# Down-projection: two of four weight block sums by adding transfers, two alternating block pairs, products in another order, and one more turn by products

## The reference, cut to what matters

```python
D_MODEL, SEQ, D_FF = 2048, 256, 5632
u_gate, u_val = u[..., :D_FF], u[..., D_FF:]
x = x + jnp.einsum('bsf,fd->bsd', jax.nn.silu(u_gate) * u_val, w_down[l])
```

## Time and profile before

| What | Value |
|---|---|
| Device time, median of 3 | 2073.01 us (2072.57 to 2073.12) |
| The profiled execution | 2072.76 us, its span 2070.8 us |
| TensorE matmul busy | 2065.6 us of 2070.8 |
| VectorE busy | 1639.7 us (79%) |
| ScalarE busy | 1162.5 us (56%) |
| GpSimd busy | 50.2 us (2%) |
| DMA queue of SP | 394.66 MB, 55.9% of 16 engines' span |
| DMA queue of GpSimd | 18.88 MB, 5.3% |
| Granted TensorE clock | 1.000 |

### The profile page before, as it was taken

How to read it: one execution, slowest core, us unless ns; L and a number is a source line. 1 busy time by engine, 2 the same in 40 slices (tenths; PEclk the granted TensorE clock), 3 DMA queues, 4 the chain that set the end, 5 groups by cost and what they waited for, 6 DMA issues and landing times.

```text
span 2070.8 us, 25481 instructions
## 1 busy us (share of the span) xinstructions
PE 2065.6 (100%) x9908; PEld 1734.6 (84%) x9908; DVE 1639.7 (79%) x1846; ACT 1162.5 (56%) x1387; POOL 50.2 (2%) x53
## 2 busy tenths in 40 slices
PE   9999999999999999999999999999999999999999
PEld 8888888888888887888888888888888888888887
DVE  7988888887888876886788668867777777789986
ACT  6766555555556555665555455555555555555553
POOL 0000000000000000110000000000000000000000
PEclk9999999999999999999999999999999999999999
DMA  9667777787774766655465556455555555556663
GB/s 344 210 200 220 226 232 225 211 245 220 247 262 151 224 207 215 204 157 189 140 231 180 201 184 221 156 185 182 191 186 192 192 193 184 193 182 235 223 206 130
DMA packets 117719, 423.28 MB, mean 204 GB/s; under 512 B 13152, under 2 KB 13920, under 8 KB 117344
## 3 DMA queue, kind: packets, MB, share of 16 engines
q1 hardware_dynamic: 109440, 394.66, 55.9%
q0 software_dynamic: 5184, 18.88, 5.3%
q10 hardware_dynamic: 2976, 8.14, 1.1%
HBM read 419.52 MB, written 2.10 MB: 204 GB/s over the span
## 4 chain that ended last, share of the span: by engine, by line
PE 99%; DMA 0%; ACT 0%; DVE 0%; ACTq 0%; issue 0%; DVEq 0%
PE g L905 52%; PE xs L951 9%; PE xs L772 8%; PE g L772 8%; PE g L955 7%; PE g L743 4%; PE xs L778 4%; PE g L778 4%; PE xs L821 1%; PE xs L992 1%; PE xs L1125 0%; PE g L930 0%; PE xs L1122 0%; DMA par<-in_params 0%; PE xs L1139 0%; PE xs L1069 0%
## 5 line engine op out<-in xcount | busy, mean ns | idle before, releaser
L1809 DVE TENSOR_TENSOR w_lo<-raw,w_hi 128x1024 fp32r<-128x1024 f32 x631 | 765.3, 1222 | 307.0 <-ACT w_hi L1322 299.6
L1322 ACT ACTIVATE w_hi<-raw 128x1024 fp32r<-128x1024 f32 x631 | 661.7, 1057 | 530.7 <-PE g L905 232.5
L905 PE MATMUL g<-w_hi,in_both 128*128 128x512 f32 x1104 | 350.6, 390 | 0.0
L905 PE MATMUL g<-w_hi,mid_both 128*128 128x512 f32 x992 | 320.3, 393 | 0.0
L905 PEld LDWEIGHTS g<-w_hi,in_both 128*128 128x128 f32 x1104 | 207.3, 188 | 42.9
L905 PEld LDWEIGHTS g<-w_hi,mid_both 128*128 128x128 f32 x992 | 186.3, 188 | 38.5
L905 PE MATMUL g<-w_lo,in_both 128*128 128x512 f32 x552 | 214.8, 389 | 0.0
L905 PE MATMUL g<-w_lo,mid_both 128*128 128x512 f32 x496 | 193.1, 389 | 0.0
L772 PE MATMUL g<-mlp_both,w_hi 128*128 128x512 f32 x704 | 167.0, 391 | 0.0
L772 PE MATMUL xs<-mlp_both,w_hi 128*128 128x512 f32 x704 | 165.6, 390 | 0.0
L772 PEld LDWEIGHTS xs<-mlp_both,w_hi 128*128 128x128 f32 x704 | 130.7, 188 | 26.2
(11 more groups left out here) (507 smaller groups left out, 3347.0 us busy)
## 6 DMA issues: line engine op xcount, KB each, us to landing
raw<-in_stream SPq DMA_DIRECT2D x631, 512.0 KB, 4.2
d_block<-in_stream SPq DMA_DIRECT2D x28, 512.0 KB, 4.3
o_block<-in_stream SPq DMA_DIRECT2D x24, 512.0 KB, 4.9
v_block<-in_stream SPq DMA_DIRECT2D x20, 512.0 KB, 4.4
ge_block<-in_stream POOLq DMA_DIRECT2D x15, 512.0 KB, 5.4
gm_block<-in_stream SPq DMA_DIRECT2D x12, 512.0 KB, 6.1
ge_block<-in_stream SPq DMA_DIRECT2D x10, 512.0 KB, 4.5
gl_block<-in_stream POOLq DMA_DIRECT2D x6, 512.0 KB, 5.4
```

The costliest lines, as they stand in the source:

```text
L905: ins = mm(GG[:, bank, :], a[:, kt, t * P:(t + 1) * P], w[:, slot, half_chunk(j)], start=n == 0 and opens(item, bank), stop=ended and n == ...
L1322: activation(w_hi[:, n % RING, :], of[:], ACT.Copy).then_inc(hi_ready, 1)
L1809: v.tensor_tensor(w_lo[:, n % RING, :], of, w_hi[:, n % RING, :].bitcast(F32), ALU.subtract).then_inc(lo_ready, 1)
```

## The change

It changes the stage `down` alone. (1) `down` joins `SPREAD`: VectorE makes two of a quad's sums (B11 + B12, and at product 2 B11 + B21 with B21 from the ring); the two with B22 are made by adding transfers that GpSimd issues. Products 3 and 2 take their blocks from the ring. (2) The four `d_block` buffers become two pairs (B11, B12) that alternate between quads; block loads are issued two quads ahead, with semaphores of their own for the second pair. (3) The order of a mixed turn becomes `MIXED_SPREAD`. (4) In group 1 turn 10 goes by products too, interleaved with the chunks of turn 8; turn 7's chunks are interleaved with the products of turn 6. Its activation sums are made at item 76, those of turn 6 still at item 64. The stage has 112 items where it had 109.

```diff
-             ((3, 0), (7, None), (4, 1), (5, 2), (8, 6), (9, None), (10, None))),
+             ((3, 0), (4, 1), (5, 2), (7, 6), (8, 10), (9, None))),
...
-SUM_TURNS = {"v": (3, 2), "out1": (4, 5), "vv": (0,), "down": (0, 1, 2, 6), "gm0": (3, 2), "out2": (1,)}
+SUM_TURNS = {"v": (3, 2), "out1": (4, 5), "vv": (0,), "down": (0, 1, 2, 6, 10), "gm0": (3, 2), "out2": (1,)}
...
-SUMS_AT = {"v": (4, 8), "out1": (2, 6), "vv": (-7,), "down": (3, 7, 11, 64), "gm0": (-8, -5), "out2": (-7,)}
+SUMS_AT = {"v": (4, 8), "out1": (2, 6), "vv": (-7,), "down": (3, 7, 11, 64, 76), "gm0": (-8, -5), "out2": (-7,)}
...
-SPREAD = ("ug", "vv", "side")
+SPREAD = ("ug", "vv", "side", "down")
+TWO_SUMS = ("vv", "side", "down")
...
 MIXED = (1, "C0", 5, 7, "C1", 6, 3, "C2", 4, 2, "C3")
...
+MIXED_SPREAD = (1, "C0", 5, "C1", 7, "C2", 6, 3, 2, "C3", 4)
...
-             FIRST_ITEM["down"] + 13: ("down", B22), FIRST_ITEM["down"] + 14: ("down", B21),
+             FIRST_ITEM["down"] + 13: ("down", B11, 1), FIRST_ITEM["down"] + 14: ("down", B12, 1),
...
+def second_pair(q):
+
+    return QUADS[q][0] == "down" and (q - quads_ahead("down")) % 2 == 1
...
 def buffer_of(q, b):
 
+    if QUADS[q][0] == "down":
+        return b + 2 * second_pair(q)
...
             for n, item in enumerate(ITEMS):
-                if next_in_place(item) is not None and quad_of(item) + 1 < len(QUADS):
-                    q = quad_of(item)
-                    if QUADS[q + 1][0] == item.phase:
+                after = 2 if item.phase == "down" else 1
+                if next_in_place(item) is not None and quad_of(item) + after < len(QUADS):
+                    q = quad_of(item) + after
+                    if QUADS[q][0] == item.phase:
                         sp.wait_ge(lo_ready, n + 1)
-                        load_block(q + 1, next_in_place(item))
+                        load_block(q, next_in_place(item))
...
-                    if item.phase in MID_ORDER and item.product == 2:
+                    if item.phase in TWO_SUMS and item.product == 2:
 
                         sp.wait_ge(sem["block_sums"], sums_made(quad_of(item), 4))
...
-                elif item.phase in MID_ORDER and item.product == 2:
+                elif item.phase in TWO_SUMS and item.product == 2:
                     dve.wait_ge(lo_ready, n + 1)
-                    to = wide(item.phase, item.group).blocks[B11]
+                    to = wide(item.phase, item.group).blocks[buffer_of(quad_of(item), B11)]
                     v.tensor_tensor(to[:], to[:], raw[:, CHUNK_COUNT[n] % RING, :], ALU.add).then_inc(sem["block_sums"], 1)
...
-                p.dma_start(wide(item.phase, item.group).blocks[to][:], stream[block_row(q, b)], accum_op=ALU.add).then_inc(
+                p.dma_start(wide(item.phase, item.group).blocks[buffer_of(q, to)][:], stream[block_row(q, b)], accum_op=ALU.add).then_inc(
```

More of the change, by code:

```diff
@@ L174 @@
         for _turn, _by_products in _steps:
-            for _what in (PLAIN if _by_products is None else MIXED_LATE if _name in ("gm1", "out2") else MIXED):
+            _mixed = MIXED_LATE if _name in ("gm1", "out2") else MIXED_SPREAD if _name in SPREAD else MIXED
+            for _what in PLAIN if _by_products is None else _mixed:
                 if _what in PLAIN:
@@ L277, in loads_of_block @@
 def loads_of_block(q, b):
-    return sum(phase not in SPREAD or b in (B11, B12) for phase, _, _ in QUADS[:q + 1])
+    return sum(not second_pair(k) and (QUADS[k][0] not in SPREAD or b in (B11, B12)) for k in range(q + 1))
+def second_pair(q):
+    return QUADS[q][0] == "down" and (q - quads_ahead("down")) % 2 == 1
 def spread_quads(q):
@@ L305, in sums_made @@
 def sums_made(q, p):
-    ahead = sum(1 if phase == "ug" else 2 if phase in MID_ORDER else 4 for phase, _, _ in QUADS[:q])
-    return ahead + ({5: 1, 4: 2} if QUADS[q][0] in MID_ORDER else {5: 1, 7: 2, 6: 3, 4: 4})[p]
+    ahead = sum(1 if phase == "ug" else 2 if phase in TWO_SUMS else 4 for phase, _, _ in QUADS[:q])
+    return ahead + ({5: 1, 4: 2} if QUADS[q][0] in TWO_SUMS else {5: 1, 7: 2, 6: 3, 4: 4})[p]
 def buffer_of(q, b):
+    if QUADS[q][0] == "down":
+        return b + 2 * second_pair(q)
     return b if b == B21 or QUADS[q][0] in SPREAD else (b + q - quads_ahead(QUADS[q][0])) % 3
@@ L569, in build @@
     down_wide = Wide(sb, "d", [("mix", 0), ("mix", 4 * kib), ("y", 88 * kib), ("y", 92 * kib)],
-                     [("h", 0), ("h", 4 * kib), ("h", 8 * kib), ("y", 12 * kib)],
-                     [("h", 12 * kib), ("h", 16 * kib), ("h", 20 * kib), ("y", 56 * kib)], ("h", 24 * kib), ("h", 28 * kib),
+                     [("h", 0), ("h", 4 * kib), ("h", 8 * kib), ("y", 12 * kib), ("y", 16 * kib)],
+                     [("h", 12 * kib), ("h", 16 * kib), ("h", 20 * kib), ("y", 56 * kib), ("y", 60 * kib)], ("h", 24 * kib), ("h", 28 * kib),
                      ("h", 24 * kib))
@@ L633, in build, with block_in @@
     block_full = [sem[f"block_full{b}"] for b in range(4)]
+    second_full = [sem[f"second_full{b}"] for b in (B11, B12)]
+    def block_in(q, b):
+        if second_pair(q):
+            return second_full[b], 16 * ((q - quads_ahead("down")) // 2 + 1)
+        return block_full[b], 16 * loads_of_block(q, b)
     hi_ready, lo_ready, mm_done = sem["hi_ready"], sem["lo_ready"], sem["mm_done"]
@@ L668, in load_block @@
                 phase, g, _ = QUADS[q]
-                sp.dma_start(wide(phase, g).blocks[buffer_of(q, b)][:], stream[block_row(q, b)]).then_inc(block_full[b], 16)
+                sp.dma_start(wide(phase, g).blocks[buffer_of(q, b)][:], stream[block_row(q, b)]).then_inc(block_in(q, b)[0], 16)
             for n, item in enumerate(ITEMS):
-                if next_in_place(item) is not None and quad_of(item) + 1 < len(QUADS):
-                    q = quad_of(item)
-                    if QUADS[q + 1][0] == item.phase:
+                after = 2 if item.phase == "down" else 1
+                if next_in_place(item) is not None and quad_of(item) + after < len(QUADS):
+                    q = quad_of(item) + after
+                    if QUADS[q][0] == item.phase:
                         sp.wait_ge(lo_ready, n + 1)
-                        load_block(q + 1, next_in_place(item))
+                        load_block(q, next_in_place(item))
                 if in_ring(item) and CHUNK_COUNT[n] + RING < len(CHUNK_ITEMS):
@@ L711, in _ @@
                         sp.wait_ge(sem["y_ready"], GROUPS)
-                    load_block(QUADS.index((phase, of[0], MID_TURN)) if of else quads_ahead(phase), b)
+                    if of and phase == "down":
+                        load_block(quads_ahead(phase) + of[0], b)
+                    else:
+                        load_block(QUADS.index((phase, of[0], MID_TURN)) if of else quads_ahead(phase), b)
                 if n in GAIN_AT:
@@ L1309, in high_of_chunk @@
                     if item.product in (1, 3, 2):
-                        act.wait_ge(block_full[b], 16 * loads_of_block(q, b))
-                    elif item.phase in SPREAD and item.product != 5 and not (item.phase in MID_ORDER and item.product == 4):
+                        act.wait_ge(*block_in(q, b))
+                    elif item.phase in SPREAD and item.product != 5 and not (item.phase in TWO_SUMS and item.product == 4):
                         act.wait_ge(sem[f"block_added{item.product}"], 16 * spread_quads(q))
@@ L1422, in first_product @@
                             act.wait_ge(sem["own_read"], own_ahead(phase, g))
-                            act.wait_ge(sem["sums_lo_ready"], sums_ahead(phase) + 4)
+                            act.wait_ge(sem["sums_lo_ready"], sums_ahead(phase) + 5)
                         own = own_banks(phase, g)
@@ L1820, in block_sums @@
                     q = quad_of(item)
-                    dve.wait_ge(block_full[B11], 16 * loads_of_block(q, B11))
-                    dve.wait_ge(block_full[B12], 16 * loads_of_block(q, B12))
+                    dve.wait_ge(*block_in(q, B11))
+                    dve.wait_ge(*block_in(q, B12))
                     dve.wait_ge(lo_ready, n + 1)
                     block_sum(item, B11, B12, B11)
-                elif item.phase in MID_ORDER and item.product == 2:
+                elif item.phase in TWO_SUMS and item.product == 2:
                     dve.wait_ge(lo_ready, n + 1)
-                    to = wide(item.phase, item.group).blocks[B11]
+                    to = wide(item.phase, item.group).blocks[buffer_of(quad_of(item), B11)]
                     v.tensor_tensor(to[:], to[:], raw[:, CHUNK_COUNT[n] % RING, :], ALU.add).then_inc(sem["block_sums"], 1)
```

## The result

The changed kernel takes **2091.12 us** (median of 4, 2088.97 to 2095.6) against 2072.91 us: ratio 1.0091, 95% interval 1.0079 to 1.0103. It is slower by 18 us, four times what was forecast (+4.3), and beyond the top of the range (2083.5).

The account below looks back on a forecast made before the run. TensorE alone was taken to bound the stage. Stalls of 2.42 + 0.84 + 1.62 + 0.8 us less 1.36 saved gave +4.3 on the profiled 2072.76, so 2077.1 us, range 2071.0 to 2083.5.

Parts of the forecast that it names:

- The costs set at nothing: SyncE's block and ring loads, the stage's last turn, and VectorE's and ScalarE's total work: no time added.
- The path: In a mixed turn: VectorE block sum, GpSimd issue, add landing, ScalarE high part, VectorE low part, then TensorE at product 7.
- the sign: The whole change makes the kernel slower, by +4.3 us.
- A loop between turns: From one mixed turn's adds to the next's: 20.6 us against 20.40, taken as 0.8 us in eight turns.
- the walk: One mixed turn timed from product 1's slot: first add issued at -1.37, landing 6.6 us, bearable up to 6.81.
- the 0.84 us at product 6: Turn with sums at item 76: sums follow C2's low part, so product 6's comes late, 0.84 us at landing 6.6.
- The row sums: VectorE's sums at items 64 and 76 delay low parts in two mixed turns: stalls of 2.42, 0.84 and 1.62 us.
- the sum turns: The two turns with row sums at items 64 and 76, costing 3.8 + 2.2 + 1.6 us at landing 8.
- All hidden: Rival: every low part is in time, the saving shows whole, -1.36 us, 2071.4 us; chance 0.14.
- adds land as lone ones: Rival: adds land in 5.2 to 5.5 us, costing +0.7 to about +1.7 us, 2074 us; chance 0.20.
- Transfers saturate: Rival: at 90% load adds take 8 us or more, product 7 stalls every turn, +9 to +14, 2083 us; chance 0.20.
- The estimate of 3.2 us: Landing of a 512 KB GpSimd transfer, 2.0 us plus bytes over 436 GB/s; no stalls by it; prediction held rows contradict it.

Follow-up runs that it names:

- experiment 1: Changed kernel with its 16 adding transfers of the stage left out, all else the same: 2071.60 us, ratio 0.9993.
- experiment 5: Kernel of experiment 4 with the row sums made at items 74 and 85, the last of a mixed turn, not 64 and 76: 2071.34 us, ratio 0.9993.
- experiment 2: Changed kernel with the fifth turn by products of the second group undone, adding transfers, buffer pairs and new order kept: 2083.41 us, ratio 1.0048.
- experiment 7: Changed kernel with the first adding transfer of each pair (for product 7) left out, the second kept: 2074.89 us, ratio 1.0008.
- experiment 9: Changed kernel with the first adding transfer of each pair made a plain copy of the same 512 KB from the same queue: 2081.77 us, ratio 1.0038.
- experiment 10: Changed kernel, order kept, with the row sums at items 74 and 85 instead of 64 and 76: 2088.93 us, ratio 1.0078.
- experiment 4: Changed kernel with mixed-turn order 1, 5, C0, C1, 3, C2, 7, 6, 2, C3, 4, so products 7 and 6 stand later: 2073.67 us, ratio 1.0004.
- experiment 8: Changed kernel with the second adding transfer of each pair (for product 6) left out, the first kept: 2078.00 us, ratio 1.0024.

## Why the prediction was wrong

**Right.** The bound was read rightly: TensorE, at 0.2267 us a matmul, 1.36 us to be had. The medians of experiments 1 and 5 lie within 0.15 us of it. The costs set at nothing (SyncE's loads, the end, VectorE's totals) were nothing, by experiment 1. The path was right, block sum, issue, add, high part, low part, and so was the sign. The first adds landed in 5.9, 7.7, 9.2, 5.9, 5.8, 6.2, 6.8 and 6.7 us, median 6.5, where I took 6.6; the two slow ones are beyond the 6.81 that product 7 bears, and one is beyond the 8 that I kept.

**The step that failed is "A loop between turns", put at 0.8 us in eight turns.** Two sizes in it were too small. The first is the landing of the second add, 7.7 us. It came from the one row of a pair beside a ring load. Measured were, one by one, 7.7, 8.8, 10.6, 11.1, 9.3, 8.4, 8.4 and 9.0, mean 9.2. The pair of the third turn as the profile lists it (issued at 1923.13 and 1925.49), the slowest first add and the second one behind it:

```profile
d_block<-in_stream POOLq DMA_DIRECT2D x1, 512.0 KB, 9.2
...
d_block<-in_stream POOLq DMA_DIRECT2D x1, 512.0 KB, 10.6
```

The loop, with the text's own steps, is 20.6 us at a landing of 7.7 and 20.6 + 1.5 = 22.1 us at 9.2, against 20.40: 1.7 us a turn, by this mean an estimate of 13.6 us for eight. The trace shows how it works. A late second add leaves VectorE late, and the next turn's first add is issued later: at 0.4 us ahead of product 1's slot in the third and the last four turns (2007.41 for a product 1 at 2007.85 in the sixth), where the walk has 1.37. That takes 0.9 us off what the first add may take and some 0.6 us off the second. In place of the 0.8 us (and the 0.84 us at product 6 that stand under the row sums) the trace has stalls of 9.9 us at products 7 and 6 and 1.8 us in four small ones behind them.

The second size is the spread of the first add. The 7.7 us in the second turn cost 0.8 us, the 9.2 us in the third 3.3 us and the first fall of the clock. A walk with one landing for all turns has no place for that.

The row I took the second landing from was of a stage where such pairs stand 42 us or more apart; here they follow every 20 us, amid eight loads. I worked out that load, 90%, and did not carry it into the landing of the second add, but gave it to a rival of its own with a chance of 0.20. Even that rival was capped too low, at +14: its own terms (7.6 us for the sum turns, 0.3 to 1.3 us in eight turns, less 1.36) add up to +8.7 to +16.7.

One turn has a cause that the walk left out. In the first turn of group 1 VectorE also works off the products of the group that has ended, and the second add is issued 3.4 us behind the first:

```profile
1957.36 0.86 POOL L2566 DMA_DIRECT2D d_block<-in_stream  x1 [31.00 <-DVE d_block L1836]
1960.76 0.86 POOL L2566 DMA_DIRECT2D d_block<-in_stream  x1 [2.54 <-DVE w_lo L1831]
```

It is the slowest add of the kernel (11.1 us), and that of this turn is the slowest in experiments 2, 7, 9 and 10 too (11.1, 7.6, 9.1 and 11.5). Why it lands so late wasn't tried.

**The row sums** were charged 4.9 us in two turns (2.42 + 0.84 + 1.62). The stalls stand where the walk puts them and in its size: 2.5 us at C2 of the turn at item 64, 1.7 us at C3 of the turn at item 75. For the first of them that is partly luck: its add landed in 5.8 us, not 6.6, and was issued 0.95 us later than in the walk. Yet moving the sums gave back only about 2.2 us (experiment 10), because other waits for adds grew in that run, up to 3.9 us at a product 6. In experiment 4, with hardly anybody waiting for adds, moving them gave 2.3 us (2073.67 to 2071.34).

**The clock** was no term at all. It fell twice, behind stalls of 3.0 and 2.2 us, for 3.4 us more.

**The rivals.** "All hidden" and "adds land as lone ones" fell: no first add of the changed kernel landed under 5.8 us. "Transfers saturate" named the mechanism best, stalls by the loop between turns, if not in every turn (the first lost nothing). But its word "saturate" isn't borne out. In experiment 5 the engines carry the same adds at no lower pace, a DMA share of 0.80 over 164 us (the 90% of the prediction was too high), and TensorE waits 0.4 us in the whole stage:

```profile
1896.00:2060.00 164.00, 164.00 (x724) 135.53 (x723) 136.92 (x129) 91.06 (x90) 12.10 (x14) 1.00 0.80 240
```

The changed kernel has 0.77 in the same stretch. The engines' total load was not the limit; the place of products 7 and 6 in the turn was. In the changed kernel, even in a turn whose issues are on time, they stand 9.5 and 10.8 us after the issues of their adds (slots 8.16 and 12.24 less issues at -1.37 and +1.4). In the order of experiment 4 it is 13.6 and 12.4 us (12.24 and 13.60 less -1.37 and about +1.2). Of that some 2.7 us go to both split parts and the hand-over, so the adds had 6.8 and 8.1 us, and now have 10.9 and 9.7. Seven of the eight second adds of the changed kernel took longer than 8.1 us; in experiment 5 the longest took 8.6. So two things went together: the products came later and the adds landed sooner (median of all 16: 5.6 us in experiment 5). Why the landings grow once stalls have begun, whether by loads that bunch behind a held ScalarE, was not tried by itself and stays open.

The estimate of 3.2 us by the fit of the Trainium skill ("DMA: Bandwidth & Descriptors", Anatomy of one DMA) holds for no add here, the least is 5.1. The plain copies of experiment 9 came near it at best, 3.6 us, but four of the eight took 7.0 us or more.

## What to carry to other kernels

An asynchronous helper (here an add by transfer in place of a VectorE sum) cost nothing where its consumer stood beyond its slowest landing, and more than it saved where its consumer stood near the median. Place consumers by the slowest landing measured in the same traffic, second of a pair included. A wait in an engine's ordered stream delays all that follows, so a late transfer that recurs each turn is priced by the period of the loop through it, not by its slack in one turn. Where a saving is 1.4 us, try the order of the items first: one line of order and one of places turned +18 us into -1.5 us. And try the parts of a change one by one: the fifth turn without the adds gave -0.8 us with one line of places.

## What the runs showed of the hardware

- An adding transfer of 512 KB from GpSimd's queue lands in 5.1 us at best, a plain copy from that queue in 3.6 (experiment 9). Of two adds 2.4 us apart the second took 5.7 to 8.6 us in experiment 5, and up to 10.6 in the changed kernel.
- Two adds cost more than twice one: 19.5 us over the kernel without adds for the pair, 6.4 and 3.3 us for either alone (experiments 1, 7 and 8).
- After a pause of 3.0 us of TensorE its granted clock was 0.50 for a while, with matmuls 0.43 us apart, and 0.23 us apart some 3.5 us later: nearly 2 us on top of the stall. Shorter pauses go either way in the profiled executions. Behind 2.24 us (changed kernel), 2.27 us (experiment 2) and 2.32 us (experiment 9) the clock fell to 0.50; behind 2.26 us (changed kernel) and 2.24 us (experiment 2) it stayed at 1.00. The Trainium skill ("TensorE: Matmul & The Clock Gate", What's actually happening) says that the throttled state is the default and activity releases it; the trace agrees, the clock came back while matmuls ran.
- Kernels near such an edge scatter: with the first adds left out, ten executions ran from 2071.6 to 2078.1 us, while the eleven of experiment 5, with hardly a wait, stayed within 1.1 us. The kernel before spread over 2.6 us in 25 executions, so part of a scatter has other causes.
